# Second model's output weights loaded inside the mixers, output norm by token halves, reordered state space stage, expert gather from a split copy

## Chip, cores and metric

One NeuronCore of one Trainium2 chip runs the whole program. The metric is the device time of one execution in microseconds (us), the median over the runs shown. PE is TensorE, DVE is VectorE, ACT is ScalarE, POOL is GpSimd and SP the engine that issues most DMAs.

## What is computed

A block of a state space and convolution mixer with an expert lookup, and then two layers of a second model, for 256 tokens of 1024 columns. Three places matter here.

```
# first block: state space mixer (16 heads of 64 in 4 groups, state 128, both directions)
dt = softplus(dt_raw + dt_bias);  a = -exp(a_log) * dt
y  = (C B^T * exp(segsum(a))) (x*dt)  +  C state * exp(cumsum a)  +  x * d_skip
o  = group_rmsnorm(y * silu(z)) * ssd_norm

# second model, for l in 0, 1
x = x + concat(ya, yb, yc) @ w_out[l]                    # rwkv, attention, gmlp
h = rms_norm(x, ffn_norm_g[l])
x = x + swiglu(h)            if l == 0
x = x + moe_swiglu(h)        if l == 1                   # 8 experts, 2 per token
# moe: logits = h @ router; top 2; gates = softmax; each expert only over its own tokens
```

## The kernel before

The program is a chain of stages with a barrier of all engines between them (class Stage, L105 to L119): inp, ssd, hy, route, exp, final, then for each of two layers z (norm and input projection), rw (stage_mixers), omix (stage_project_norm, L1354) and dense (l = 0) or moe (l = 1). Within a stage each engine has its own instruction list, written out by hand, and waits on semaphores; the order in those lists sets the order of the work. SP's list is a queue too: a DMA behind a wait is issued after it.

**ssd** (stage_ssd, L659). SP loads two tables for dt and a_log, the triangular masks tri, d_skip and the norm row (L705 to L709). PE turns 10 blocks of the convolved input (L723), while DVE makes softplus and a (L892 to L915); then PE makes the cumulative sums (L733) and the same as rows, once for output partitions 0 and once for 32 (L740). DVE weights x into xw (L930). Then PE: state_of(0), gates_of(0), the row sums of heads 0 and 2, off_of(0), and a loop over 16 heads: sums_of broadcasts the rows of a later head, DVE's head_in makes a difference, ACT its exponential, DVE's head_mask the matrices Mf and Mb (L953, L954), and PE's head_out multiplies them with xw (L784). All heads of a group of 4 collect in one bank py. group_out (L975) adds it to the skip term (L979, which frees py), adds the state's part and multiplies with z; it stands behind the masks of head 4g + 5. At the end the squares, one root, and eight scalings (L1018) go before four blocks of transposes (L814) and copies (L884).

**rw** (stage_mixers, L2109) holds three tiles X, Y and Z3 for the attention. After the last values product (L2319, semaphore m_o_psum) X, Y and Z3 hold nothing that is read again.

**omix** (stage_project_norm). SP loads w_out in two halves of 2 MB, each after the one before has landed (L1375). PE multiplies oT with each half for both token halves: four pieces of 8 products of 512 columns (L1388), an fp32 product being two instructions. DVE adds each to x_tok (L1426). After all four come the squares of both token halves (L1407), the root, the scaling to xn (L1444), 16 transposes (L1397) and 8 scalings to hT (L1454).

**moe** (stage_moe, L2863). Start: SP loads the router, stores x_tok to the output rows, loads three tables and the first two weight blocks (L2951 to L2958). PE's router products (L2981) and DVE's work wait for all four tables. DVE finds the top 2, each token's slot, the list of passes (L3174 to L3197), and then the matrix Pg of ones and zeros that picks the tokens of a pass (L3202). PE gathers them: xn times Pg in fp32 (L2999), over 8 row blocks and 2 token halves. DVE multiplies with the norm gain into hE (L3207), ACT makes its high part hEh (L3079) and DVE the low part hEl (L3212). A pass streams 84 weight blocks through a ring of 21: ACT makes the high part, DVE the low part (fp32r, a 32 bit type for which a product is one instruction), and PE makes six products of 512 columns with each (L3019, L3037). Near its end it gathers the next pass's tokens. Nine passes run.

## Time and profile before

| | us |
|---|---|
| median of 3 runs | 3401.13 |
| lowest, highest | 3394.55, 3401.63 |
| profiled execution, its own time | 3392.16 |
| its span, first to last instruction | 3390.3 |
| ssd stage | 117 |
| omix0, omix1 | 49, 50 |
| moe before its first expert product | 34 |
| moe from there to the end | 1114 |

The page's part 1 has the busy time of each engine, part 4 the chain of work that ended last, followed back from the last instruction. In the timeline the bracket gives the idle time of the engine before an instruction and what released it. PEclk is the granted TensorE clock: 1.0 is 2.4 GHz, 0.5 is 1.2 GHz. The forms print fp32r operands of products as f32; L3019, L3037 and L2008 have fp32r operands, L2999 and all of ssd and omix fp32.

### The profile page before, as it was taken

The numbers are of one execution on the slowest core, as the hardware profiler recorded it, in microseconds if no ns is written. First come the engines' busy times: TensorE is split into PE (matmuls) and PEld (weight loads), VectorE is DVE, ScalarE is ACT, GpSimd is POOL, SyncE is SP. The second block draws the span as 40 slices with busy tenths as digits, with TensorE's granted clock in tenths as the row PEclk, the third lists the DMA queues.
The fourth block names the chain that finished last, engine by engine and source line by source line (L and its number), as shares of the span: only waits on it lengthen the run. The fifth ranks groups of instructions, "written<-read, shape, count | busy, mean of one in ns | idle before, by whom it ended". The sixth has DMA issues, their size and how long they took to land. (4 is left out here: it accounts for less than half of the span.)

```text
span 3390.3 us, 49857 instructions
## 1 busy us (share of the span) xinstructions
PE 3086.4 (91%) x17008; PEld 2570.3 (76%) x17009; DVE 2437.8 (72%) x3650; ACT 1755.2 (52%) x2184; POOL 41.5 (1%) x47
## 2 busy tenths in 40 slices
PE   7998798888899999977879987779999999999997
PEld 3796546888788999965849866648888888888886
DVE  3665663889788666658635467539889999998996
ACT  3343203436533444435224344128888887887886
POOL 0000000000000000000000000000000000000000
PEclk9998698999999999988989988879999999999999
DMA  7560143444577766521045240059999999999994
GB/s 273 203 225 29 40 165 106 133 150 180 218 247 223 220 212 212 187 114 46 1 178 180 104 150 1 31 214 377 376 349 379 372 355 379 362 364 358 386 360 179
DMA packets 225854, 731.95 MB, mean 216 GB/s; under 512 B 23527, under 2 KB 59800, under 8 KB 222872
## 3 DMA queue, kind: packets, MB, share of 16 engines
q1 hardware_dynamic: 221784, 702.32, 56.8%
q0 software_dynamic: 2768, 23.59, 2.4%
q10 hardware_dynamic: 1152, 4.19, 0.3%
q8 instruction: 74, 1.21, 0.1%
q14 instruction: 76, 0.62, 0.1%
HBM read 702.24 MB, written 28.84 MB: 216 GB/s over the span
## 5 line engine op out<-in xcount | busy, mean ns | idle before, releaser
L3216 DVE TENSOR_TENSOR moe_lo<-moe_raw,moe_hi 128x1024 fp32r<-128x1024 f32 x756 | 886.0, 1220 | 55.3 <-ACT moe_hi L3069 36.1
L3069 ACT ACTIVATE moe_hi<-moe_raw 128x1024 fp32r<-128x1024 f32 x756 | 788.1, 1061 | 147.9 <-PE moe_pB L3019 78.0
L3019 PE MATMUL moe_pB<-moe_hi,moe_hEh 128*128 128x512 f32 x1008 | 399.7, 397 | 3.8 <-DVE moe_hEl L3212 3.8
L3019 PE MATMUL moe_pB<-moe_hi,moe_hEl 128*128 128x512 f32 x1008 | 394.1, 391 | 0.0
L3019 PE MATMUL moe_pB<-moe_lo,moe_hEh 128*128 128x512 f32 x1008 | 393.5, 390 | 0.0
L1531 PE MATMUL route_pS<-fh,route_uh 128*128 128x256 f32 x640 | 191.3, 299 | 35.4 <-DVE route_ul L1634 35.1
L3019 PEld LDWEIGHTS moe_pB<-moe_hi,moe_hEh 128*128 128x128 f32 x1008 | 190.0, 188 | 41.6 <-issue 4.0
L3019 PEld LDWEIGHTS moe_pB<-moe_hi,moe_hEl 128*128 128x128 f32 x1008 | 189.7, 188 | 40.7
L3019 PEld LDWEIGHTS moe_pB<-moe_lo,moe_hEh 128*128 128x128 f32 x1008 | 190.1, 189 | 37.9
L1866 PE MATMUL exp_pO<-exp_vh,exp_ah 128*128 128x512 f32 x512 | 201.0, 393 | 4.4 <-DVE exp_al L1925 4.4
L1866 PE MATMUL exp_pO<-exp_vl,exp_ah 128*128 128x512 f32 x512 | 200.6, 392 | 0.0
L1866 PE MATMUL exp_pO<-exp_vh,exp_al 128*128 128x512 f32 x512 | 199.9, 390 | 0.0
L3037 PE MATMUL moe_pB<-moe_hi,moe_ah 128*128 128x512 f32 x504 | 197.0, 391 | 0.0
L3037 PE MATMUL moe_pB<-moe_hi,moe_al 128*128 128x512 f32 x504 | 196.2, 389 | 0.0
L3037 PE MATMUL moe_pB<-moe_lo,moe_ah 128*128 128x512 f32 x504 | 196.1, 389 | 0.0
L1889 ACT ACTIVATE exp_vh<-exp_vs 128x1024 fp32r<-128x1024 f32 x128 | 135.2, 1056 | 116.5 <-PE exp_pO L1866 94.3
L1914 DVE TENSOR_TENSOR exp_vl<-exp_vs,exp_vh 128x1024 fp32r<-128x1024 f32 x128 | 156.3, 1221 | 41.2 <-ACT exp_vh L1889 39.7
L1531 PE MATMUL route_pS<-fl,route_uh 128*128 128x256 f32 x640 | 185.2, 289 | 0.0
L1531 PE MATMUL route_pS<-fh,route_ul 128*128 128x256 f32 x640 | 185.0, 289 | 0.0
L1531 PEld LDWEIGHTS route_pS<-fh,route_uh 128*128 128x128 f32 x640 | 126.8, 198 | 40.2 <-DVE route_ul L1634 29.9
L1854 PE MATMUL exp_pS<-fh,exp_ul 128*128 128x256 f32 x512 | 144.9, 283 | 0.0
L1854 PE MATMUL exp_pS<-fl,exp_uh 128*128 128x256 f32 x512 | 144.9, 283 | 0.0
(742 smaller groups left out, 6738.8 us busy)
## 6 DMA issues: line engine op xcount, KB each, us to landing
moe_raw<-in_moe_w SPq DMA_DIRECT2D x758, 512.0 KB, 6.4
exp_vs<-in_peer_v SPq DMA_DIRECT2D x128, 512.0 KB, 4.6
route_us<-in_peer_u SPq DMA_DIRECT2D x64, 512.0 KB, 3.5
exp_us<-in_peer_u SPq DMA_DIRECT2D x64, 512.0 KB, 5.2
inp_w<-in_w_mod SPq DMA_DIRECT2D x48, 512.0 KB, 6.2
inp_w<-in_w_tiles SPq DMA_DIRECT2D x40, 512.0 KB, 6.0
gates<-route_big POOLq DMA_DIRECT2D x8, 2048.0 KB, 7.5
exp_gs<-gates SPq DMA_DIRECT2D x32, 512.0 KB, 5.8
```

The lines of the kernel that those rows point to most:

```text
L1531: m = pe.matmul(pS[:, n % 2, 0:T], w, x[:, kd], start=kd == 0 and q == 0, stop=kd == KD - 1 and q == 2)
L1854: m = pe.matmul(pS[:, j % 2, 0:T], w, x[:, kd], start=kd == 0 and q == 0, stop=kd == KD - 1 and q == 2)
L1866: m = pe.matmul(pO[:, a, h], w[:, j % RING, ts], x, start=False, stop=False, skip_group_check=True)
L1889: act.activation(vh[:, j % RING], vs[:, j % RING], ACT.Copy).then_inc(vh_ready, 1)
L1914: dve.tensor_tensor(vl[:, j % RING], vs[:, j % RING], vh[:, j % RING], ALU.subtract).then_inc(vl_ready, 1)
L3019: i = pe.matmul(pB[:, kind], l[:, kd], m[:, n % HALVES, ns], start=kd == 0 and x == 0, stop=kd == KD - 1 and x == 2)
L3037: i = pe.matmul(pY[:, h], l[:, u], m[:, n % HALVES, hs], start=g == 0 and u == 0 and x == 0, stop=g == GROUPS - 1 and u == UNITS - 1 and x ...
L3069: act.activation(hi[:, n % HALVES], raw[:, n % RING], ACT.Copy).then_inc(hi_ready, 1)
L3216: dve.tensor_tensor(lo[:, n % HALVES], raw[:, n % RING], hi[:, n % HALVES], ALU.subtract).then_inc(lo_ready, 1)
```

## The change

- ssd: the dt, a_log and d_skip tables are loaded in the inp stage; tri is the stage's first load. gates_of(0) stands among the first transposes, DVE's gates(0) behind a. The row sums go in pairs to partitions 0 and 32. state_of(0) comes after the sums of heads 0 and 2, off_of(0) after head 1. The read of py is a function of its own (inner), ahead of the mask of the next group's first head. The first three groups are normed before the last group's output, and transposed as each is ready.
- mixers and omix: X, Y and Z3 become parts of one allocation that lives until omix ends, and w_out is loaded into it once m_o_psum is reached. The new stage_omix goes by token halves: the four pieces in the order of the token half, each token half squared, normed, turned and scaled by itself, the transposes of the first one between pieces 3 and 4. The scalings of the transposed blocks are shared by DVE and ACT. In layer 1 the norm gain is multiplied into xn as a row, and the transposed blocks are only copied.
- moe: xn, which now has the gain in it, is split once into xh and xl (fp32r), a second matrix Pz is made in fp32r, and the gather is the sum of the products of xh and xl with Pz. hE and its product fall out. The router has a semaphore of its own; the store of x_tok comes after the first two weight blocks; the first Pg and Pz are made before the pass list.

```diff
+                for dst, src in tables["loads"]:
+                    sp.dma_start(dst, src).then_inc(tables["loaded"], 16)
...
-        sp.dma_start(dtb[:], dt_bias.rearrange("a b h -> (a b h)").partition_broadcast(P)).then_inc(dt_loaded, 16)
-        sp.dma_start(alog[:], a_log.rearrange("a b h -> (a b h)").partition_broadcast(P)).then_inc(dt_loaded, 16)
         sp.dma_start(tr[:], tri).then_inc(tri_loaded, 16)
-        sp.dma_start(dskip[:], d_skip.rearrange("a h -> (a h)").partition_broadcast(P)).then_inc(nrm_loaded, 16)
         sp.dma_start(nrm[:], norm.rearrange("a h -> (a h)").partition_broadcast(P)).then_inc(nrm_loaded, 16)
...
+        def gates_of(g):
+            if g:
+                pe.wait_ge(state_ready, g + 1)
+            for s in range(TT):
+                i = pe.matmul(pg[:, s * T:(s + 1) * T], xbcT[:, 8 + g, s * P:(s + 1) * P], xbcT[:, 12 + g, 0:T], start=True, stop=True)
+            i.then_inc(g_psum, 1)
...
+            if n == 1:
+                gates_of(0)
...
-        for base in (0, 32):
-            for d, half, terms in ((0, 0, [(LE, 0)]), (0, 1, [(None, 0), (LE, 1)]), (1, 1, [(GE, 1)]), (1, 0, [(GE, 0), (None, 1)])):
-                at = d * T + half * P
-                for nt, (which, src) in enumerate(terms):
+        for d, half, terms in ((0, 0, [(LE, 0)]), (0, 1, [(None, 0), (LE, 1)]), (1, 1, [(GE, 1)]), (1, 0, [(GE, 0), (None, 1)])):
+            at = d * T + half * P
+            for nt, (which, src) in enumerate(terms):
+                for base in (0, 32):
                     i = pe.matmul(prow[base:base + HEADS, at:at + P], a[:, src, d * HEADS:(d + 1) * HEADS],
                                   k.ones[:] if which is None else tr[:, which], start=nt == 0, stop=nt == len(terms) - 1)
...
         def state_of(g):
             pe.wait_ge(xw_ready, 1 + g // 2)
+            pe.wait_ge(g_ready, max(g, 1))
             if g == 0:
                 pe.wait_ge(x_read, 10)
-            else:
-                pe.wait_ge(g_ready, g)
+            if g == 1:
+                pe.wait_ge(state_ready, 1)
             for s in range(TT):
                 i = pe.matmul(pg[:], btok[:, s, g, :], xw[:, TT + s, g].rearrange("p d n -> p (d n)"), start=s == 0, stop=s == TT - 1)
             i.then_inc(state_psum, 1)
-        def gates_of(g):
...
-        state_of(0)
-        gates_of(0)
         pe.wait_ge(row_ready, 1)
         pe.wait_ge(ea_ready, 1)
         pe.wait_ge(na_cum, 1)
         sums_of(0)
         sums_of(2)
-        off_of(0)
+        state_of(0)
...
-            if h % HPG == 1 and g:
+            if h % HPG == 1:
                 off_of(g)
...
-            pe.wait_ge(o_ready, n // 2 + 1)
+            pe.wait_ge(o_ready, n + 1)
...
-        keep_state(0)
...
+            if h == 0:
+                keep_state(0)
...
+        act.wait_ge(mean_ready, 1)
+        act.activation(rt[:, 0:LAST], ms[:, 0:LAST], ACT.Sqrt).then_inc(root_ready, 1)
         squares(GROUPS - 1)
-        act.wait_ge(mean_ready, 1)
-        act.activation(rt[:], ms[:], ACT.Sqrt).then_inc(root_ready, 1)
+        act.wait_ge(mean_ready, 2)
+        act.activation(rt[:, LAST:], ms[:, LAST:], ACT.Sqrt).then_inc(root_ready, 1)
...
+        gates(0)
...
+        def inner(g):
+            dve.wait_ge(y_psum, (g + 1) * HPG)
+            dve.tensor_tensor(y[:, :, g * H4:(g + 1) * H4], py[:].rearrange("p (l n) -> p l n", l=TT), xd[:], ALU.add).then_inc(py_read, 1)
...
-        dve.wait_ge(nrm_loaded, 32)
-        skipped(0)
-        gates(0)
+        dve.wait_ge(nrm_loaded, 16)
         head_in(0)
...
             if hh == 0 and g:
                 gates(g)
+                inner(g - 1)
             head_mask(h)
+            if h == 0:
+                skipped(0)
...
+        def normal(first, last, cols):
+            dve.wait_ge(squared, last * TT)
+            dve.tensor_scalar(ms[:, cols], ss[:, cols], 1.0 / H4, EPS, ALU.mult, ALU.add).then_inc(mean_ready, 1)
+            dve.wait_ge(root_ready, 1 if first == 0 else 2)
+            c.link(dve.reciprocal(rs[:, cols], rt[:, cols]))
+            for g in range(first, last):
+                gs = slice(g * H4, (g + 1) * H4)
+                for l in range(TT):
+                    i = dve.scalar_tensor_tensor(out=y[:, l, gs], in0=y[:, l, gs], scalar=rs[:, g * TT + l:g * TT + l + 1],
+                                                 in1=nrm[:, gs], op0=ALU.mult, op1=ALU.mult)
+                i.then_inc(o_ready, 1)
+
+        normal(0, GROUPS - 1, slice(0, LAST))
+        inner(GROUPS - 1)
         group_out(GROUPS - 1)
...
+        normal(GROUPS - 1, GROUPS, slice(LAST, TT * GROUPS))
...
+        sp.wait_ge(q["m_o_psum"], 1)
+        for h in range(2):
+            sp.dma_start(w_out[:, h], w_tiles[h]).then_inc(w_loaded, 16)
...
+PIECES = [(a, h) for a in range(TT) for h in range(2)]
...
+        pe.wait_ge(w_loaded, 32)
+        for a, h in PIECES:
+            for kd in range(KD):
+                i = pe.matmul(pm[a][h][:], oT[:, kd, a * P:(a + 1) * P], w[:, h, kd], start=kd == 0, stop=kd == KD - 1)
+            i.then_inc(mix_psum, 1)
+            if (a, h) == (1, 0):
+                turned(0)
+        turned(1)
...
+    @block.vector
+    def _(dve):
+        c = Chain(dve, ch)
+
+        def added(n):
+            a, h = PIECES[n]
+            hs = slice(h * BANK, (h + 1) * BANK)
+            dve.wait_ge(mix_psum, n + 1)
+            dve.tensor_tensor(x_tok[:, a, hs], pm[a][h][:], x_tok[:, a, hs], ALU.add).then_inc(x_ready, 1)
+
+        def normed(a):
+            dve.wait_ge(squared, 2 * a + 2)
+            c.link(dve.tensor_tensor(xms[:, a:a + 1], xss[:, a, 0:1], xss[:, a, 1:2], ALU.add))
+            dve.tensor_scalar(xms[:, a:a + 1], xms[:, a:a + 1], 1.0 / D, EPS, ALU.mult, ALU.add).then_inc(mean_ready, 1)
+            dve.wait_ge(root_ready, a + 1)
+            c.link(dve.reciprocal(xrs[:, a:a + 1], xrt[:, a:a + 1]))
+            dve.wait_ge(x_ready, 2 * a + 2)
+            if row is None:
+                dve.tensor_scalar(xn[:, a], x_tok[:, a], xrs[:, a:a + 1], None, ALU.mult).then_inc(xn_ready, 1)
+            else:
+                dve.wait_ge(row_loaded, 16)
+                dve.scalar_tensor_tensor(out=xn[:, a], in0=x_tok[:, a], scalar=xrs[:, a:a + 1], in1=rowt[:],
+                                         op0=ALU.mult, op1=ALU.mult).then_inc(xn_ready, 1)
+
+        def scaled(a):
+            dve.wait_ge(t_psum, 2 * a + 1)
+            if row is not None:
+                i = dve.tensor_copy(hT[:, 0:4, a * P:(a + 1) * P], pt[0][:].rearrange("p (j t) -> p j t", t=P))
+            else:
+                for kd in range(4):
+                    i = dve.tensor_scalar(hT[:, kd, a * P:(a + 1) * P], pt[0][:, kd * P:(kd + 1) * P], scales[:, kd:kd + 1], None, ALU.mult)
+            i.then_inc(t_read_dve, 1)
+
+        added(0)
+        added(1)
+        normed(0)
+        added(2)
+        scaled(0)
+        added(3)
+        normed(1)
+        scaled(1)
...
-        sp.dma_start(rw[:], router).then_inc(loaded, 16)
-        sp.dma_start(rows[0:T].rearrange("(a p) d -> p a d", p=P), x_tok[:]).then_inc(x_kept, 16)
+        sp.dma_start(rw[:], router).then_inc(rw_loaded, 16)
...
+        sp.dma_start(rows[0:T].rearrange("(a p) d -> p a d", p=P), x_tok[:]).then_inc(x_kept, 16)
...
-        pe.wait_ge(loaded, 64)
+        pe.wait_ge(rw_loaded, 16)
...
+        pe.wait_ge(loaded, 48)
...
-                for a in range(TT):
-                    i = pe.matmul(pX[:, half, n * P:(n + 1) * P], xn[:, a, kd * P:(kd + 1) * P], Pg[:, a], start=a == 0, stop=a == TT - 1)
+                for x, src in enumerate((xh, xl)):
+                    for a in range(TT):
+                        i = pe.matmul(pX[:, half, n * P:(n + 1) * P], src[:, a, kd * P:(kd + 1) * P], Pz[:, a],
+                                      start=x == 0 and a == 0, stop=x == 1 and a == TT - 1)
...
+        pe.wait_ge(xl_ready, 1)
...
+        act.activation(xh[:], xn[:], ACT.Copy).then_inc(xh_ready, 1)
...
-            act.wait_ge(hE_ready, p + 1)
-            act.activation(hEh[:], hE[:], ACT.Copy).then_inc(hEh_ready, 1)
+            act.wait_ge(gather_psum, 2 * p + 2)
+            act.activation(hEh[:].rearrange("p k t -> p (k t)"), pX[:].rearrange("p b n -> p (b n)"), ACT.Copy).then_inc(hEh_ready, 1)
...
-        dve.wait_ge(loaded, 64)
+        dve.wait_ge(xh_ready, 1)
+        dve.tensor_tensor(xl[:], xn[:], xh[:], ALU.subtract).then_inc(xl_ready, 1)
+        dve.wait_ge(loaded, 48)
...
+        def gather_matrix(p):
+            for a in range(TT):
+                dve.tensor_scalar(Pg[:, a], io[:], slot[:, a, bass.ds(p, 1)], None, ALU.is_equal)
+                i = dve.tensor_scalar(Pz[:, a], io[:], slot[:, a, bass.ds(p, 1)], None, ALU.is_equal)
+            i.then_inc(pg_ready, 1)
...
+        gather_matrix(0)
...
-            dve.tensor_tensor(hE[:].rearrange("p (b k) t -> p b k t", b=2), pX[:].rearrange("p b (k t) -> p b k t", k=4),
-                              scales.rearrange("p (b k) -> p b k", b=2).unsqueeze(3).to_broadcast([P, 2, 4, P]), ALU.mult).then_inc(hE_ready, 1)
...
-            dve.tensor_tensor(hEl[:], hE[:], hEh[:], ALU.subtract).then_inc(h_ready, 1)
+            dve.tensor_tensor(hEl[:].rearrange("p k t -> p (k t)"), pX[:].rearrange("p b n -> p (b n)"),
+                              hEh[:].rearrange("p k t -> p (k t)"), ALU.subtract).then_inc(h_ready, 1)
...
-        gather_matrix(0)
...
+    shared = keep(heads, f"heads{l}", [P, 3 * 2 * BHEADS * T], "right")
+    w_out = shared[:, 0:2 * KD * BANK].rearrange("p (h k n) -> p h k n", h=2, k=KD)
+    w_loaded = nc.alloc_semaphore(f"w_out_loaded{l}")
```

## Rows read from the trace of the kernel before

**Rows 1.** Page, part 4: chain that ended last, shares of the span by engine
```profile
PE 33%; DMA 0%; DVE 0%; ACT 0%; issue 0%; SPq 0%; ACTq 0%; POOL 0%; POOLq 0%; DVEq 0%
```

**Rows 2.** Windows by stage: us, PE, PEld, DVE, ACT, POOL busy, PEclk, DMA share, GB/s
```profile
295.70:412.70 117.00, 89.77 (x380) 60.65 (x380) 76.66 (x162) 40.42 (x90) 0.00 (x0) 0.68 0.02 8
...
2191.10:2241.30 50.20, 33.46 (x80) 15.73 (x80) 7.91 (x16) 2.50 (x5) 0.00 (x0) 0.83 0.23 84
2241.30:2275.20 33.90, 18.28 (x78) 15.86 (x78) 13.91 (x68) 5.99 (x7) 1.51 (x3) 0.57 0.97 371
...
2397.00:2518.70 121.70, 121.70 (x570) 101.40 (x569) 110.50 (x106) 98.88 (x103) 2.16 (x2) 1.00 0.97 367
```

**Rows 3.** Timeline of omix0: start us, us, engine line op out<-in xcount [idle before <-releaser]
```profile
1699.24 8.24 SPq L1375 DMA_DIRECT2D omix_w<-in_w_out  x2
...
1707.19 29.27 PE L1388 MATMUL omix_pm<-omix_w,oT 128*128 128x512 f32 x64 [11.22 <-DMA omix_w<-in_w_out]
...
1744.93 1.73 DVE L1454 TENSOR_SCALAR hTf<-omix_pt,cols 128x256 f32<-128x256 f32 x4 [0.36 <-PE omix_pt L1397]
```

**Rows 4.** Timeline of omix1, its two weight loads (the second waits for the first)
```profile
2191.97 9.34 SPq L1375 DMA_DIRECT2D omix_w<-in_w_out  x2
```

**Rows 5.** Timeline of the mixers of layer 0, PE, last values products
```profile
1642.42 0.61 PE L2319 MATMUL rw_p<-rw_mla_v,rw_mla_y 128*128 128x64 f32 x4
```

**Rows 6.** Timeline of the state space stage, DVE, to head 0's second matrix
```profile
299.80 0.48 DVE L892 TENSOR_TENSOR ssd_u<-ssd_p,ssd_dtb 128x32 f32<-128x32 f32 x4 [12.44 <-DMA ssd_alog<-in_ssd_a_log]
...
301.35 0.36 DVE L900 COPY ssd_mf<-ssd_tri 128x128 f32<-128x128 f32 x2 [0.61 <-DMA ssd_tri<-in_tri]
...
327.65 0.68 DVE L954 TENSOR_TENSOR ssd_Mb<-ssd_ex,ssd_gb 128x512 f32<-128x512 f32 x1
```

**Rows 7.** Timeline of the state space stage, PE, sums and row sums
```profile
309.35 0.60 PE L733 MATMUL ssd_p<-ssd_a,ssd_tri 128*128 128x16 f32 x4
...
310.77 0.56 PE L740 MATMUL ssd_p<-ssd_tri,ssd_a 128*16 128x128 f32 x2
...
314.40 0.38 PE L740 MATMUL ssd_p<-ones,ssd_a 128*16 128x128 f32 x2
```

**Rows 8.** Timeline of the state space stage, PE, first head of groups 1 and 2
```profile
346.00 0.66 PE L784 MATMUL ssd_py<-ssd_xw,ssd_Mf 128*128 128x64 f32 x2 [5.04 <-DVE fT L979]
...
367.28 0.66 PE L784 MATMUL ssd_py<-ssd_xw,ssd_Mf 128*128 128x64 f32 x2 [2.90 <-DVE fT L979]
```

**Rows 9.** Timeline of the state space stage, its end
```profile
399.34 0.69 DVE L979 TENSOR_TENSOR fT<-ssd_py,ssd_xd 128x512 f32<-128x512 f32 x1 [4.04 <-PE ssd_py L784]
...
406.15 3.25 DVE L1018 SCALAR_TENSOR_TENSOR fT<-fT,ssd_rs,ssd_nrm 128x256 f32<-128x256 f32 x8
...
411.75 0.60 ACT L884 ACTIVATE oT<-ssd_p 128x512 f32<-128x512 f32 x1 [0.26 <-PE ssd_p L814]
```

**Rows 10.** Timeline of the expert stage up to its first product
```profile
2248.64 7.00 PE L2981 MATMUL moe_pX<-moe_rw,hTf 128*128 128x8 f32 x32 [3.87 <-DMA moe_tr<-in_tri]
...
2264.77 0.48 DVE L3202 TENSOR_SCALAR moe_Pg<-moe_io,moe_slot 128x128 f32<-128x128 f32 x2
...
2265.31 6.11 PE L2999 MATMUL moe_pX<-moe_Pg,xnf 128*128 128x128 f32 x32 [5.28 <-DVE moe_Pg L3202]
...
2271.45 1.23 DVE L3207 TENSOR_TENSOR moe_hE<-moe_pX,cols 128x1024 f32<-128x1024 f32 x1 [3.53 <-PE moe_pX L2999]
...
2275.26 0.79 PE L3019 MATMUL moe_pB<-moe_hi,moe_hEh 128*128 128x512 f32 x1 [3.85 <-DVE moe_hEl L3212]
```

**Rows 11.** Timeline of PE, first half of one gather
```profile
2389.94 1.95 PE L2999 MATMUL moe_pX<-moe_Pg,xnf 128*128 128x128 f32 x16
```

**Rows 12.** Chain in order of time: start us, us, products of one group
```profile
2300.64 5.44 PE moe_pB L3037 x24
```

**Rows 13.** Line L2999, weight loads: count, duration ns min/median/max
```profile
L2999 PEld LDWEIGHTS moe_pX<-moe_Pg,xnf x320: 187/192/333, 2265.3 to 3367.4; 128*128 128x128 f32 x160
```

**Rows 14.** Line L3019, weight loads of fp32r operands
```profile
L3019 PEld LDWEIGHTS moe_pB<-moe_hi,moe_hEh x1008: 187/188/331, 2275.3 to 3357.2; 128*128 128x128 f32 x168
```

More of the change, by code:

```diff
@@ L656, with stage_ssd @@
 LOG1P_TERMS = 9
-def stage_ssd(nc, k, dt_bias, a_log, d_skip, norm, tri, xbcT, z_tok, dtT, xtok, ytok, oT):
+def stage_ssd(nc, k, tables, norm, tri, xbcT, z_tok, dtT, xtok, ytok, oT):
     LE, GE, LT, GT = range(4)
@@ L2874, in stage_moe @@
+def stage_moe(nc, k, router, iota, tri, w, hT, xn, x_tok, rows, out):
     KINDS, UNITS = 3, 4
@@ L3610, in second_layer @@
         else:
-            stage_moe(nc, k, a["router"], a["iota"], a["tri"], a["moe_w"], hT, xn, k.col(f"ffn{l}"), x_tok, a["moe_rows"], out)
+            carried.close()
+            stage_moe(nc, k, a["router"], a["iota"], a["tri"], a["moe_w"], hT, xn, x_tok, a["moe_rows"], out)
 def kernel(**inputs):
```

144 lines of the change are left out of this document (92 added, 52 removed).

## Prediction

> **What bounds it now.** I read the chain that ended last first: TensorE (PE) alone holds it [rows 1], and all of that third of the span lies in the expert stage. Then the windows by stage. In one expert pass PE is busy 121.70 of 121.70 us, DVE 110.50, ACT 98.88, DMA 0.97 of the time [rows 2]: PE bounds the nine passes, with DVE and DMA close. The stages that the change touches besides are not bound by one engine: state space takes 117.0 us with PE busy 89.8 at a mean clock of 0.68 and DVE 76.7, the expert start 33.9 us with PE 18.3 [rows 2]. There the timelines say what each wait ends on. The profiled execution took 3392.2 us (span 3390.3); the median of the runs is 3401.1, nine above it. The sum is made against 3392.2 and carried over to the median.
>
> **omix0 and omix1.** SP issues the output weights at 1699.24, PE starts at 1707.19 [rows 3]; with the weights in SBUF PE starts where SP now issues: -8.0. In omix1 the first load is issued at 2191.97 and the second, which waits for the first to land as PE does, 9.0 later (9.34 less its own 0.33) [rows 4]: -9.0. The new loads wait for the last values product, done by 1643.03 [rows 5]; omix0 starts at about 1698.3, so 4 MB have 55 us where the old stage needed about 8 us for each half. SP has nothing queued behind that wait. PE started at the lower clock before and does so after: 0, or up to 2 us either way per stage. The tail: the products end at 1707.19 + 29.27 = 1736.46, the last hT piece at 1746.66 [rows 3], 10.2 us of adds, squares, root, scaling and transposes over both token halves. Afterwards only the second half is left behind the last product: 5.4 us by halving each long operation (add, square, scale) and keeping the short ones. PE does the first half's eight transposes ahead of the last 6.9 us of products, 8 x 0.11 = 0.9. So -3.9 each (-2 to -5). In omix1 the gain row makes the scaling a two-input operation (+0.5) and merges four scalings into one copy (-0.4). Both stages: -8.0 - 9.0 - 2 x 3.9 = **-24.8**, between -20 and -29.
>
> **State space.** Its first DVE operation waits until 299.80 for the a_log table; the masks then wait until 301.35 for tri [rows 6]. The three tables come with the front stage, where SP only gives 3 more small issues in a queue that mostly waits for ring space. Tri becomes the first load and the chain to the decay moves up 1.4 (0.5, if tri needs as long as now, to 2.8). The row sums, 24 instructions from 310.77 to 314.78 [rows 7], go in neighbouring pairs to output partitions 0 and 32, which may overlap: -2 (0 to -2). The sums of heads 0 and 2 no longer stand behind the state product, its copy and the gates, which are computed earlier; DVE's own weighting ends 1.4 earlier, and head 0's matrices, ready at 328.33 [rows 6], come some 10 us earlier. PE does not keep that: state 0, two heads, state 1 and the state's contribution of group 0 now stand between, mostly at the low clock. Adding them (2.9, 2 x 2.6, sums 1.9, 3.4, 3.4, then 1.35 + 0.9 + 1.1 + 1.35 at the high one) from 315.4 on gives head 3 out at 337, the drained bank and head 4's matrices (0.7 + 1.3) at 339, against 346.00 [rows 8]: -7. In the later groups PE waited 2.90 until the bank was drained, behind two mask pairs [rows 8]; draining comes first now, but then waits for the heads of the group before and delays the mask by 0.7: -0.8 for each of two groups. The end: 13.0 us from the last product's drain at 399.34 to 412.35 [rows 9]. Six of the eight scalings (3.25 x 6/8 = 2.4) and the table load move into the 4.04 us that DVE idled; they overrun it by 0.6. Left: 8.9, so -4.1. Sum 7.0 + 1.6 + 4.1 = **-12.7**, between -5 (PE stays at the low clock through group 0) and -19.
>
> **Expert start.** The router products waited 3.87 us, for tri, queued behind 1 MB of x_tok [rows 10]; they need only the router now, and x_tok goes behind the first two weight blocks. I take -2.8, as their low parts on DVE come next. ACT's split copy and DVE's subtraction over 2048 columns (2 x 1.2 us) run while DVE waited for the same tables. PE waited 5.28 us for the gather matrix [rows 10]; the pass list (4 us of small operations) moves behind it, while four comparisons instead of two (0.48 for two [rows 10]) stay: -3.7. The gather, 6.11 us because its end ran at the high clock, runs fully at the low one: +0.9. The 1.23 us product with the scales falls out [rows 10]: -1.2. Sum **-6.8**, between -3 and -11. The weight ring starts the passes with some 15 blocks instead of 20 in it, still enough, as SP's waits in the passes are for ring space, not the reverse. POOL's wait for x_tok ends long before its first scatter.
>
> **The gather in the passes** is the disputed price. Before: 16 fp32 products are 32 instructions, two halves of 16 in 1.95 us [rows 11]. Sixteen of 128 columns in 1.95 and four of 16 columns in 0.60 [rows 7] give the same spacing: 1.35/12 = 0.112 us, whatever the columns. So the weight load sets it. After: 32 fp32r instructions. Their load lasts 188 ns as that of the fp32 ones, 192 [rows 13, 14], and 24 fp32r products of 512 columns take 5.44 us, 227 each [rows 12], 13 more than 512/2.4 = 213. The trace has no fp32r product under 256 columns, so I bound it: below by 128/2.4 + 13 = 66 ns, above by four trips of the columns, 213 + 13 = 227. I take 112 to 120, by the equal loads: 0 to +0.26 per pass, **+1** in nine passes. DVE loses 1.23 and gains two comparisons (0.5) per pass, under PE. The Trainium skill, "TensorE: Matmul & The Clock Gate", section "Back-to-back issue gap", has a stream of load and product at 128 columns settle at about 81 ns; by it the gather would fall by 32 x 31 ns, 1 us a pass. The rows of this trace stand at 112 for fp32.
>
> **Sum.** -24.8 - 12.7 - 6.8 + 1 = -43, so 3349 for the profiled kind of execution and **3358 us** for the median.
>
> **Rivals.**
> (a) *Light loads*: fp32r weights load faster than rows 14 suggest, 66 ns per instruction: 9 x 32 x 0.046 = -13, and -3 in the first gather, 3342. The Trainium skill, "TensorE: Matmul & The Clock Gate", section "Weight-path perf modes", has the fast weight load on for 128 weights that are not FP32; fp32r may be such a type. Against: the equal load durations.
> (b) *Narrow fp32r runs at a quarter rate*: 227 ns. 9 x 32 x 0.115 = +33 and up to +4 in the first gather, so -6 in all: 3395, no change. For it: nothing narrower than 256 was ever split here. Against: no row.
> (c) *The clock*: the gather now streams half the columns per instruction (one trip of 128, not two), and PE in the state space stage fell to the low clock with thin products, to a mean of 0.68 [rows 2]. If it falls in each gather, 1.5 to 3 us a pass: +13 to +27, about 3378. Against: the gather is 4 us between products of 512 columns.
> (d) *The other side, slower*: narrow fp32r at a quarter rate with its weight load not hidden, 227 + 107 = 334 ns. 9 x 32 x 0.222 = +64, +6 at the start: 3401 - 44 + 70 = 3427. It decides from 0.112 + 44/320 = about 250 ns per gather instruction on. For it: PE is bound, so every ns shows. Against: all fp32r loads in the trace hide.
> (e) *The change does less than it says*: PE at the low clock in omix and group 0, tri late: all terms at their small ends, -28 + 3, 3376.
>
> **Chances.** Forecast 0.55, (a) 0.12, (b) 0.11, (c) 0.08, (d) 0.04, (e) 0.10. A measurement here can tell about 0.2% (7 us) from no change. Of (b), 0.02 falls faster, 0.08 within and 0.01 slower. Faster 0.55 + 0.12 + 0.08 + 0.10 + 0.02 = 0.87, same 0.08, slower 0.04 + 0.01 = 0.05. The range runs from 3336 (the forecast with its large ends, (a) in it) to 3382 ((e), and most of (c)); (b) and (d) are left out, 0.15.
>
> **What would show it.** omix0 and omix1: first product under 1 us behind the barrier, no wait for weights, 5 to 6 us from last product to end; stages of about 37 us. State space near 104 us, head 4 some 7 us earlier, scalings between head 15's matrices and the last drain. Expert start 27 us. A pass of 121.7 to 122.0 with 32 gather instructions: 112 to 120 ns apart says the load sets it, 66 to 81 says (a), 227 or a doubled count says (b), 334 (d), a clock of 0.5 in the passes (c). The forecast falls if the pass changes by over 1 us, or if omix still shows a wait for DMA.

## The result and the profile after

The changed kernel took 3351.16 us (median of 4 runs, 3345.71 to 3357.79), the kernel before on the same chip 3398.49: a ratio of 0.9862, with a 95% interval of 0.984 to 0.9884, 47 us. The profiled execution took 3357.79 us (span 3356.1), the slowest of the four. Against the 3392.16 of before it gained 34.4 us only, so a part of the gain lies in what differs from one execution to the next. A later series gave 3350.60 against 3396.11, 45.5 us.

The chain that ended last is still PE's [rows 1], with the same 33% of the span.

The windows of the same stages, columns as in [rows 2] (state space, omix1, expert start, one pass):

```profile
296.00:402.70 106.70, 89.15 (x380) 61.25 (x380) 76.98 (x164) 40.03 (x91) 0.00 (x0) 0.69 0.02 8
2174.60:2212.30 37.70, 32.11 (x80) 15.06 (x80) 7.57 (x14) 4.49 (x12) 0.00 (x0) 0.91 0.04 14
2212.30:2241.30 29.00, 16.63 (x79) 14.29 (x79) 15.23 (x70) 7.99 (x8) 1.51 (x3) 0.56 0.92 348
2362.00:2483.64 121.64, 121.64 (x570) 101.38 (x569) 109.68 (x107) 99.17 (x103) 1.84 (x2) 1.00 0.97 366
```

By the barriers between the stages (the windows are rounded), state space takes 106.70 us instead of 116.92, omix0 37.36 instead of 48.66, omix1 37.70 instead of 50.24, the expert start 28.95 instead of 33.97, a pass 121.64 instead of 121.706. Together -39.7, of -34.4 in all: some 5 us came back elsewhere (dense +2.4 and route +1.3, which the change does not touch, norm and mixers of layer 1 +1.8). The stages vary by that much from one execution to the next: in the two executions of before, dense took 199.8 and 202.0 us. So 34.4 us is not the gain, and the medians are what counts.

**omix**, its timeline, with the load of w_out as SP issues it in the mixers of layer 0 (answers to [rows 3]):

```profile
1633.74 0.80 SPq L2263 DMA_DIRECT2D heads<-in_w_out  x2
```

```profile
1689.97 22.92 PE L2915 MATMUL omix_pm<-heads,oT 128*128 128x512 f32 x48 [3.33 <-PEq L119]
...
1713.60 7.03 PE L2915 MATMUL omix_pm<-heads,oT 128*128 128x512 f32 x16
...
1720.67 0.69 DVE L2953 TENSOR_TENSOR x_tok<-omix_pm,x_tok 128x512 f32<-128x512 f32 x1 [6.02 <-PE omix_pm L2915]
...
1724.90 1.14 ACT L2928 ACTIVATE hTf<-omix_pt,cols 128x128 f32<-128x128 f32 x4 [2.17 <-PE omix_pt L2909]
```

PE starts 1.0 us behind the barrier at 1688.99, with no wait for a transfer. Its last product ends at 1720.63, the last hT piece at 1726.04: 5.4 us, as the prediction had it, instead of 10.2. omix1 has 6.2, as its last eight transposes ran at the low clock (1.91 us for them, 1.09 in omix0):

```profile
2209.48 1.91 PE L2909 MATMUL omix_pt<-ident,xnf 128*128 128x128 f32 x8 [3.67 <-DVE xnf L2966]
...
2211.43 0.60 ACT L2930 ACTIVATE hTf<-omix_pt 128x512 f32<-128x512 f32 x1 [3.52 <-PE omix_pt L2909]
```

In the one execution where they ran at the high clock there (below, output weights in omix again), the tail of omix1 is 5.4 us too.

**State space**, PE and DVE, to the first head of group 1 (answers to [rows 7, 8]) and at the end (to [rows 9]):

```profile
311.65 0.62 PE L749 MATMUL ssd_p<-ssd_tri,ssd_a 128*16 128x128 f32 x4
...
313.76 0.64 PE L749 MATMUL ssd_p<-ones,ssd_a 128*16 128x128 f32 x4
...
340.65 0.69 PE L789 MATMUL ssd_py<-ssd_xw,ssd_Mf 128*128 128x64 f32 x2 [2.08 <-DVE ssd_Mb L972]
```

```profile
391.38 2.46 DVE L1030 SCALAR_TENSOR_TENSOR fT<-fT,ssd_rs,ssd_nrm 128x256 f32<-128x256 f32 x6
...
393.76 0.68 DVE L983 TENSOR_TENSOR fT<-ssd_py,ssd_xd 128x512 f32<-128x512 f32 x1
...
401.82 0.60 ACT L890 ACTIVATE oT<-ssd_p 128x512 f32<-128x512 f32 x1 [0.26 <-PE ssd_p L817]
```

The row sums take 2.75 us for 24 instructions (311.65 to 314.40), the first head of group 1 starts 44.6 us behind the barrier instead of 50.3, and the waits of 5.04 and 2.90 are now 2.08, for the masks and not for the bank. (In the nine other executions of this code that head starts 38.4 to 41.7 us behind the barrier.) The last drain starts at 393.76, the stage's work ends at 402.42: 8.7 us.

**Expert start** (answers to [rows 10]):

```profile
2216.46 3.75 PE L3108 MATMUL moe_pX<-moe_rw,hTf 128*128 128x8 f32 x32
...
2222.11 1.06 ACT L3205 ACTIVATE moe_hi<-moe_raw 128x1024 fp32r<-128x1024 f32 x1 [7.07 <-DMA moe_raw<-in_moe_w]
2223.20 2.59 DVE L3289 TENSOR_TENSOR moe_lo<-moe_raw,moe_hi 128x1024 fp32r<-128x1024 f32 x2 [5.34 <-ACT moe_hi L3205]
...
2225.71 0.17 DVE L3291 COPY moe_lg<-moe_pX 128x16 f32<-128x16 f32 x1
...
2231.60 0.66 PE L3128 MATMUL moe_pX<-moe_Pz,moe_xh 128*128 128x128 f32 x2 [1.55 <-DVE moe_Pz L3310]
...
2239.83 1.23 DVE L3346 TENSOR_TENSOR moe_hEl<-moe_pX,moe_hEh 128x1024 fp32r<-128x1024 f32 x1 [1.48 <-ACT moe_hEh L3211]
...
2241.29 0.79 PE L3149 MATMUL moe_pB<-moe_hi,moe_hEh 128*128 128x512 f32 x1 [2.63 <-DVE moe_hEl L3346]
```

The router's products no longer wait. But they end at 2220.21, and DVE reads them at 2225.71: its queue has the first two low parts ahead, and those wait for the first weight block. They stood there before the change too, as two rows of that trace show:

```profile
2252.82 2.50 DVE L3155 TENSOR_TENSOR moe_lo<-moe_raw,moe_hi 128x1024 fp32r<-128x1024 f32 x2 [3.62 <-ACT moe_hi L3073]
...
2255.67 0.17 DVE L3157 COPY moe_lg<-moe_pX 128x16 f32<-128x16 f32 x1 [0.35 <-PE moe_pX L2981]
```

There the low parts ended at 2255.32, and DVE waited only 0.35 us more for the router's products.

**The gather** in a pass and its weight loads (answers to [rows 11, 13]):

```profile
2356.36 0.33 PE L3128 MATMUL moe_pX<-moe_Pz,moe_xh 128*128 128x128 f32 x2
...
2358.10 0.62 PE L3156 MATMUL moe_pT<-ident,moe_prod 128*128 128x128 f32 x4
```

```profile
L3128 PEld LDWEIGHTS moe_pX<-moe_Pz,moe_xh x160: 187/192/333, 2231.6 to 3333.0; 128*128 128x128 f32 x160
```

Sixteen fp32r products in 2358.10 - 2356.36 = 1.74 us, 109 ns each on average and mostly 112 from one to the next, the spacing of the fp32 ones. The clock is at 1.0 throughout. From the first gather product of a pass to the expert product behind the last one are 3.93 us, before the change (2389.94 to 2393.87) and after (2356.36 to 2360.29).

### The profile page after: what moved, and what is told of

It reads as the page before. It is cut to its first block and busy times, and to the rows that moved or that the text cites. A ratio compares the mean times of both kernels' runs of the same rounds, so it can differ in the third digit from the quotient of the medians.

```text
span 3356.1 us, 49912 instructions
## 1 busy us (share of the span) xinstructions
PE 3086.5 (92%) x17008; PEld 2574.3 (77%) x17009; DVE 2430.1 (72%) x3665; ACT 1762.9 (53%) x2206; POOL 39.8 (1%) x47
## 5 line engine op out<-in xcount | busy, mean ns | idle before, releaser
L1882 PE MATMUL exp_pO<-exp_vh,exp_al 128*128 128x512 f32 x512 | 199.8, 390 | 0.0
```

Of the source, the lines that this page charges most:

```text
L1882: m = pe.matmul(pO[:, a, h], w[:, j % RING, ts], x, start=False, stop=False, skip_group_check=True)
```

## The experiments

All are edits of the changed kernel. Nine with a question of their own come first, then two executions for comparison and a version put together.

**Row sums apart.**

```diff
-for d, half, terms in (...):
+for base, d, half, terms in [(base, *t) for base in (0, 32) for t in (...)]:
     at = d * T + half * P
     for nt, (which, src) in enumerate(terms):
-        for base in (0, 32):
...
```

> The changed kernel with the row sums of the state space stage in their old order (all for output partitions 0, then all for 32). In the changed kernel the 24 of them took 2.75 us at the low clock, 115 ns apart, where single fp32 instructions at that clock stand 213 apart. Theory: neighbours that write to partitions 0 and 32 overlap, so undone they take about 24 x 0.213 = 5.1 us at the low clock (or some 4.0 if the clock rises in between), and head 0 of group 1 and the stage come 1.3 to 2.4 us later. Rival: a short instruction costs half as much in any order there; then the stage stays within 0.3 us of 106.7.

PE's timeline, first and last row sums:

```profile
310.82 0.61 PE L749 MATMUL ssd_p<-ssd_tri,ssd_a 128*16 128x128 f32 x2
...
314.61 0.64 PE L749 MATMUL ssd_p<-ones,ssd_a 128*16 128x128 f32 x2
```

4.43 us (310.82 to 315.25) instead of 2.75, both at the low clock, so neighbours for partitions 0 and 32 do overlap: in the changed order the two of a pair start 7 ns apart and the next pair 213 ns after the first. The Trainium skill, "TensorEngine Tiling (Array Packing)", section "Key Properties", says that different tiles can execute in parallel; these rows agree. The stage, though, took 102.90 us, and three executions of the unedited stage with the same mean clock of 0.71 took 102.59, 102.60 and 103.26. The 1.7 us were gone by the first head of group 1 (41.35 us behind the barrier, 41.2 to 41.7 in those three), so what the pairs gained for the stage is too small to be measured. The rival's 0.3 us around 106.7 was set on one execution; against the right neighbours the stage did not change. The clock mattered more than the order: in the second execution of the kernel before, the old order ran at the high clock and took 2.37 us.

**Bank read late again.**

```diff
 if hh == 0 and g:
     gates(g)
-    inner(g - 1)
...
 if hh == 1 and g:
+    inner(g - 1)
     group_out(g - 1)
```

> The changed kernel with the read of py behind the mask of head 4g + 5 again. Theory: that read is what PE waits for at each of the three group changes, and it now comes two pairs of mask and difference later: PE's wait of 2.08 us in front of heads 4, 8 and 12 grows to 2.9 or more, the stage by 0.8 to 1.7 us at each change, 3 to 5 in all, to about 111. Rival: PE's clock and the exponentials set the pace of the groups, and the read is hidden: the stage within 1 us of 106.7.

```profile
337.96 0.41 PE L789 MATMUL ssd_py<-ssd_xw,ssd_Mf 128*128 128x64 f32 x2 [3.26 <-DVE fT L983]
...
358.06 0.41 PE L789 MATMUL ssd_py<-ssd_xw,ssd_Mf 128*128 128x64 f32 x2 [2.90 <-DVE fT L983]
...
378.18 0.66 PE L789 MATMUL ssd_py<-ssd_xw,ssd_Mf 128*128 128x64 f32 x2 [2.90 <-DVE fT L983]
```

The waits grew from 2.08 to 3.26, 2.90 and 2.90, 2.8 us in sum, as the theory had it. The stage took 102.56 us at a mean clock of 0.72. The executions of the unedited stage at 0.73 took 99.8 to 100.5, those at 0.71 took 102.6 to 103.3, so between them about 101.3 would be due: 1 to 1.5 us is left of the 3 to 5 expected. From the first product of head 4 to the last product of the stage this execution took 51.36 us, and two of the unedited stage with the same clock there (0.70) took 49.80 and 49.85: the two later waits cost what they grew by, 1.64. So the theory had the waits right and the price of each (0.8 to 1.7 us) too high; and the rival, that the read is hidden, is wrong by this comparison.

**Output weights in omix again.**

```diff
-sp.wait_ge(q["m_o_psum"], 1)
-for h in range(2):
-    sp.dma_start(w_out[:, h], w_tiles[h]).then_inc(w_loaded, 16)
...
+for h in range(2):
+    sp.dma_start(w[:, h], w_tiles[h]).then_inc(w_loaded[h], 16)
...
-pe.wait_ge(w_loaded, 32)
+if a == 0:
+    pe.wait_ge(w_loaded[h], 16)
```

> The changed kernel with both halves of w_out issued at the start of omix0 and omix1 instead of in the mixers, one semaphore for each half, the work by token halves kept. Theory: PE starts 8 us later and the second half, issued at once behind the first, lands within PE's 7 us of the first piece: omix0 and omix1 each 8 to 9 us longer, 45.5 to 46.5 us. Rival: the transfer in the mixers slows something there or in the stage before; then the mixers of this run are shorter than 165.4 and 181.3 us, by up to several us, and what was gained in omix is partly only moved.

omix0 took 45.28 us (+7.9) and omix1 46.90 (+9.2). SP and PE in omix0:

```profile
1684.90 0.81 SPq L2895 DMA_DIRECT2D heads<-in_w_out  x2
...
1693.00 22.40 PE L2915 MATMUL omix_pm<-heads,oT 128*128 128x512 f32 x48 [11.38 <-DMA heads<-in_w_out]
```

The first half needs 8.1 us, and the second is there in time. The mixers took 166.99 and 176.69 us, values that executions with the load in the mixers also had (167.01 and 176.75): moving the 4 MB there cost nothing that can be seen. (Those executions vary, from 165.4 to 169.4 and from 176.7 to 181.3 us, so a cost of a us or two would be seen only in such close pairs.)

**Norm of both halves behind the last product.**

```diff
-        if (a, h) == (1, 0):
-            turned(0)
+    turned(0)
     turned(1)
...
-    act.wait_ge(x_ready, n + 1)
+    act.wait_ge(x_ready, 4)
...
-added(0); added(1); normed(0); added(2); scaled(0); added(3); normed(1); scaled(1)
+added(0); added(1); added(2); added(3); normed(0); normed(1); scaled(0); scaled(1)
```

> The changed kernel with nothing of the norm started before the fourth piece (weights still loaded in the mixers). Theory: what stands behind the last product is again all of squares, root, scalings, 16 transposes and their copies: 10 us instead of 5.4 (omix0) and 6.2 (omix1), less the 0.9 of transposes that PE no longer does ahead: both stages 3 to 4.5 us longer, 40.5 to 42. Rival: with ACT and DVE sharing the copies the tail is short in any order, and the stages grow by less than 2.

omix0 41.21 us (+3.9), omix1 40.48 (+2.8). The end of omix0:

```profile
1718.21 0.69 DVE L2951 TENSOR_TENSOR x_tok<-omix_pm,x_tok 128x512 f32<-128x512 f32 x1 [6.17 <-PE omix_pm L2915]
...
1727.28 1.14 ACT L2927 ACTIVATE hTf<-omix_pt,cols 128x128 f32<-128x128 f32 x4 [2.87 <-PE omix_pt L2909]
```

From the last product (its add starts at 1718.21) to 1728.42 are 10.2 us, just the tail of before. So the gain in the tail is that of the work by token halves. In omix1 it is less, as there the tail of the changed kernel is 6.2.

**Gather with 64 columns.**

```diff
-for x, src in enumerate((xh, xl)):
...
+pieces = [(0, P)] if n % 2 == 0 else [(0, P // 2), (P // 2, P)]
+for lo_, hi_ in pieces:
+    for x, src in enumerate((xh, xl)):
...
```

> The changed kernel with every second block of the gather done in two halves of 64 columns: 16 instructions of 128 columns and 32 of 64 in a gather, the result the same. Theory: the weight load sets the spacing, whatever the columns (110 to 112 ns): the gather takes 48 x 0.111 = 5.3 us instead of 4.1, and as PE bounds the passes each is 1.8 us longer, 123.4, the kernel 16 us. Rival: the columns set it: 64 columns 55 to 66 ns apart, the gather 3.6 to 4.1 us as before, the pass 121.6.

One pass, and eight instructions of 64 columns (x2 four times) in a gather:

```profile
2360.00:2483.46 123.46, 123.46 (x585) 103.16 (x585) 109.70 (x106) 99.18 (x103) 1.77 (x2) 1.00 0.96 361
```

```profile
2351.22 0.36 PE L3130 MATMUL moe_pX<-moe_Pz,moe_xh 128*128 128x64 f32 x2
...
2352.09 0.42 PE L3130 MATMUL moe_pX<-moe_Pz,moe_xh 128*128 128x128 f32 x2
```

2352.09 - 2351.22 = 0.87 us for eight, 109 ns on average at 64 columns as at 128. The pass took 123.46 us (+1.82), the execution 3368.59. So the columns do not set the spacing. That the weight load does fits, as each instruction has one of its own, but it was not varied here. The row sums of the state space stage have loads of 16 columns instead of 128; in the second execution of the kernel before they ran at the high clock:

```profile
L740 PEld LDWEIGHTS ssd_p<-ssd_tri,ssd_a x16: 92/97/97, 310.3 to 312.1; 128*16 128x16 f32 x16
```

Their loads take 97 ns instead of 192, and their fp32 products of 128 columns still start 109 ns apart. So for fp32 at 128 columns a shorter load does not shorten the spacing; for fp32r, what sets it stays open. The Trainium skill, "TensorE: Matmul & The Clock Gate", section "Back-to-back issue gap", has about 81 ns at 128 columns; the trace differs, and it decides.

**Gather in fp32.**

```diff
-for x, src in enumerate((xh, xl)):
-    for a in range(TT):
-        i = pe.matmul(pX[...], src[:, a, ...], Pz[:, a], ...)
+for a in range(TT):
+    i = pe.matmul(pX[...], xn[:, a, ...], Pg[:, a], ...)
...
-act.activation(xh[:], xn[:], ACT.Copy).then_inc(xh_ready, 1)
```

> The changed kernel with the gather in fp32 from xn and Pg again (the gain still multiplied into xn before; no xh, xl, Pz). Theory: an fp32 product is two instructions of the same spacing as one fp32r instruction, so the pass is the same within 0.1 us (121.64), and the expert start the same or up to 1 us shorter, since four comparisons become two (0.4) and DVE's xl (2.3 us) was hidden. Rival: the split gather saves PE time: then a pass with the fp32 gather is longer by 0.5 us or more.

The pass is 121.71 us again (+0.07), the start 26.89, 1.4 to 2.2 less than with the split gather (28.29 to 29.12 in the others), more than the theory's 0 to 1. Two comparisons fewer are 0.5 of it. The rest is the clock, which rose inside this gather, as in both executions of before; it took 5.67 us instead of 7.06:

```profile
2223.50 5.67 PE L3126 MATMUL moe_pX<-moe_Pg,xnf 128*128 128x128 f32 x32 [1.07 <-DVE moe_Pg L3301]
```

**Low parts later.**

```diff
-for n in range(PRE):
-    dve.wait_ge(hi_ready, n + 1)
-    dve.tensor_tensor(lo[:, n], raw[:, n], hi[:, n], ALU.subtract).then_inc(lo_ready, 1)
 dve.wait_ge(l_psum, 1)
...
 gather_matrix(0)
+for n in range(PRE):
+    dve.wait_ge(hi_ready, n + 1)
+    dve.tensor_tensor(lo[:, n], raw[:, n], hi[:, n], ALU.subtract).then_inc(lo_ready, 1)
```

> The changed kernel with DVE's low parts of the first two weight blocks behind the gather matrix instead of ahead of the read of the router's products. In the changed kernel the router's products end at 2220.2, DVE reads them at 2225.7, because it waits for the first block (landed 2222.1) and makes two low parts. Theory: the read comes at once, everything up to the first expert product moves 5.4 us forward: the start takes 23.5 us instead of 28.95. Rival: the first weight blocks are late anyway, or their low parts stand in front of the last step: less than 3 us gained, and the first expert product waits for a low part.

```profile
2216.38 0.17 DVE L3288 COPY moe_lg<-moe_pX 128x16 f32<-128x16 f32 x1 [1.96 <-PE moe_pX L3108]
...
2229.38 1.02 ACT L3211 ACTIVATE moe_hEh<-moe_pX 128x1024 fp32r<-128x1024 f32 x1 [8.24 <-PE moe_pX L3128]
...
2231.57 1.23 DVE L3346 TENSOR_TENSOR moe_hEl<-moe_pX,moe_hEh 128x1024 fp32r<-128x1024 f32 x1 [0.25 <-DVE moe_meta L3330]
...
2233.03 0.79 PE L3149 MATMUL moe_pB<-moe_hi,moe_hEh 128*128 128x512 f32 x1 [3.68 <-DVE moe_hEl L3346]
```

The router's products are read 7.9 us behind the barrier (2208.47) instead of 13.4, and the first expert product starts at 24.56 us, 4.4 earlier (5.4 expected; the rival had less than 3). The missing 1.1 us is a new wait: the low part of the gathered tokens (2231.57) now starts behind the gates' arithmetic on DVE, 1.17 us after ACT's high part ended at 2230.40.

**Store of x_tok first.**

```diff
 sp.dma_start(rw[:], router).then_inc(rw_loaded, 16)
+sp.dma_start(rows[0:T]..., x_tok[:]).then_inc(x_kept, 16)
...
-sp.dma_start(rows[0:T]..., x_tok[:]).then_inc(x_kept, 16)
```

> The changed kernel with the store of x_tok (1 MB) ahead of the three tables and the first weight blocks, as before the change; the router's own semaphore is kept. Theory: the store takes DMA time ahead of the first block, which lands 2 to 4 us later, and DVE's read of the router's products behind it: the start 2 to 4 us longer than 28.95. Rival: the router's semaphore alone gave the gain; the start within 0.5 us of 28.95.

```profile
2213.45 1.17 SPq L3085 DMA_DIRECT2D moe_raw<-in_moe_w  x2
...
2218.27 1.06 ACT L3205 ACTIVATE moe_hi<-moe_raw 128x1024 fp32r<-128x1024 f32 x1 [6.88 <-DMA moe_raw<-in_moe_w]
```

The start is 28.74 us, unchanged. The weight blocks are issued 4.8 us behind the barrier (2208.69) instead of 2.2 to 2.6, and ACT has the first at 9.6 us. In the other eleven executions it had it at 8.9 to 10.4 us, in the two of before at 9.6 and 10.4. The rival was right. Why an earlier issue brings no earlier landing stays open.

**PE kept at work.**

```diff
 i.then_inc(l_psum, 1)
+for n in range(8):
+    pe.matmul(pY[:, n % 2], k.zero[:], hT[:, 0:2, :], start=True, stop=True)
...
 i.then_inc(rank_psum, 1)
+for n in range(1):
+    pe.matmul(pY[:, n % 2], k.zero[:], hT[:, 0:2, :], start=True, stop=True)
```

> The changed kernel with PE kept at work in the expert start: eight more zero products of 512 columns between the router's products and the ranks (where PE waited 7.5 us), and one between the ranks and the gather (where it waited 1.55 us). They write zeros where zeros already stand. Theory: PE was at the low clock through the ranks (2.3 us) and the gather (7.06 us) because it had only waited or streamed 8 columns at a time before; with the 512-column products the clock is at 1.0 there, the ranks take 1.2 us and the gather 3.6 to 4.1: the start 3.5 to 4.5 us shorter than the 28.3 to 28.95 us of the runs so far. Rival: the clock falls again in the ranks and in the wait behind them; the gather still takes over 6 us and the start is the same within 0.5 us, or up to 0.5 longer.

```profile
2219.33 0.28 PE L3115 MATMUL moe_pX<-moe_chosen,moe_tr 128*128 128x8 f32 x2
...
2226.71 1.02 ACT L3215 ACTIVATE moe_hEh<-moe_pX 128x1024 fp32r<-128x1024 f32 x1 [10.26 <-PE moe_pX L3132]
...
2229.07 1.23 DVE L3350 TENSOR_TENSOR moe_hEl<-moe_pX,moe_hEh 128x1024 fp32r<-128x1024 f32 x1 [0.25 <-DVE moe_meta L3334]
```

The clock did most of what the theory said: the ranks took 1.2 us instead of 2.3, and the gather 4.6 instead of 7.06 at a mean clock of 0.79, not the 3.6 to 4.1 of a clock of 1.0. The start, 27.96 us, hardly moved, as the rival had it, for another reason. The eight products overran, so that the ranks began 2.0 us late, and the low part of the tokens waited 1.3 us for the gates' arithmetic on DVE. These two took back 3.3 of the 3.6 us gained on PE.

**The kernel before, once more.**

> The kernel before the change, unchanged, to see what its state space stage does in another execution. In seven executions of one and the same code of the changed stage it took 96.96 to 106.70 us, and the longer the clock was low in it (46.8 to 67.1 us) the longer it took, about 0.48 us for each us. Theory: the stage of before has the same swing (116.92 us with 74.4 us low was near its long end), so another execution may well give a shorter one, on a line of the same slope: 110 to 117 us. Rival: the old order holds the clock down always: within 1 us of 116.9. The passes, omix and the expert start stay within 0.3 us of 121.71, 48.7, 50.2 and 34.0 in either case.

```profile
295.98:410.57 114.59, 85.65 (x380) 57.92 (x380) 76.50 (x162) 40.18 (x90) 0.00 (x0) 0.72 0.02 8
```

114.59 us instead of 116.92, mean clock 0.72 instead of 0.68. That lies in the expected 110 to 117, but not on the expected line: 10.2 us less at the low clock (64.3 instead of 74.5) were worth 2.3 us, 0.23 for each. The passes (121.71) and the expert start (34.17) repeated within 0.2 us, omix0 (49.2) and omix1 (49.7) to about half a us, where 0.3 was expected.

**The changed kernel, once more**, five rounds.

> The changed kernel, unchanged, as the measure for the next run and to see which of its profile's stages repeat. Theory: omix0 37.4, omix1 37.7, the pass 121.64 and the gather of the start 7.06 repeat within 0.2 us (omix0 within 0.6), the expert start within 0.7; the state space stage does not, and lands between 97 and 107 us on a line with the time at the low clock. Median 3346 to 3357 us. Rival: the 106.7 us of its first profile is the rule, and the shorter ones of the experiments came from their edits.

Median 3350.60 us (3348.72 to 3351.57) against 3396.11, ratio 0.9864 (0.9849 to 0.9879). omix0 37.87, omix1 37.70, expert start 29.12, pass 121.64, all as expected. The rival, that 106.7 us is the rule for the state space stage, is refuted. That stage here, and the same code at its fastest, in the kernel with the weights loaded in omix:

```profile
295.90:396.50 100.60, 81.64 (x380) 55.78 (x380) 77.02 (x164) 39.95 (x91) 0.00 (x0) 0.73 0.03 9
```

```profile
297.71:394.68 96.97, 80.69 (x380) 55.00 (x380) 77.06 (x164) 40.07 (x91) 0.00 (x0) 0.76 0.03 9
```

In all twelve executions of the changed kernel and its edits, time and mean clock of this stage go together:

| mean clock | stage, us | stage code |
|---|---|---|
| 0.76 | 96.97 | changed |
| 0.73 | 99.76, 99.83, 99.88, 99.94, 100.54 | changed |
| 0.71 | 102.59, 102.60, 103.26 | changed |
| 0.69 | 106.70 | changed |
| 0.72 / 0.71 | 102.56 / 102.90 | bank read late / row sums apart |
| 0.72 / 0.68 | 114.59 / 116.92 | before |

So order and clock can be told apart in part. Before, with 64.3 us at the low clock, the stage took 114.59; between its executions with 60.4 us (103.26) and 67.1 (106.70) the changed stage would take about 105.3 (an estimate from these rows). Some 9 us are the new order at an equal clock. The other 5 of the mean difference go with less time at the low clock, 56 us on average instead of 69; two executions of before are too few to say that this belongs to the change.

**A start put together**: the low parts later and the gather in fp32, as in the two edits above, two zero products ahead of the ranks and one behind them, and the gates' arithmetic (choices) last.

```diff
-choices()
 gathered(0)
+choices()
```

> The changed kernel with the expert start put together from what the runs showed: low parts of the first two blocks behind the gather matrix, the gates' arithmetic behind the low part of the gathered tokens, the gather in fp32 as before the change, two zero products in PE's wait before the ranks and one behind them. Theory: router read at 7.9 us, gather from about 13.7 for 4 to 5.7 us, its two parts 2.4 us more: the first expert product 21 to 22.5 us behind the barrier instead of 28.3, the pass 121.71 (+0.6 in nine), the kernel 5 to 7 us below the changed one. Rival: the gates' arithmetic now delays the third block's low part and the token numbers, PE waits in the first pass instead, and less than 3 us is left.

```profile
2214.25 0.17 DVE L3284 COPY moe_lg<-moe_pX 128x16 f32<-128x16 f32 x1 [2.32 <-PE moe_pX L3107]
...
2219.80 3.84 PE L3130 MATMUL moe_pX<-moe_Pg,xnf 128*128 128x128 f32 x32
...
2226.23 1.22 DVE L3341 TENSOR_TENSOR moe_hEl<-moe_pX,moe_hEh 128x1024 fp32r<-128x1024 f32 x1 [0.22 <-DVE moe_passi L3333]
...
2227.69 0.49 PE L3150 MATMUL moe_pB<-moe_hi,moe_hEh 128*128 128x512 f32 x1 [4.05 <-DVE moe_hEl L3341]
...
2232.88 0.19 PEld L3150 LDWEIGHTS moe_pB<-moe_hi,moe_hEh 128*128 128x128 f32 x1 [1.03 <-DVE moe_lo L3346]
```

The start is 21.72 us, 7.4 less than in the run beside it, the gather 3.84 at the high clock. The median is 3342.01 us (3339.49 to 3344.57) against 3350.60 (3348.72 to 3351.57) for the changed kernel in the same series; the runs do not overlap, and the difference is 8.6 us where 5 to 7 were expected. Against before the ratio is 0.9838 (0.9824 to 0.9851). The rival showed in small: PE waits 0.59 us in the first pass for a low part, and the low part of the tokens still stands 1.5 us behind the pass list.

## Why the prediction was right, point by point

The forecast was -43 us; the two series have -47.3 and -45.5, inside the range. The total came out nearer than its terms. As measured over the executions they are about -23.8, -14.5, -5.4 and -0.6, together -44; the state space stage and the gather gave 1.8 and 1.6 us more than forecast, omix and the expert start 1.0 and 1.4 less, and that these cancel is luck. The forecast for the profiled kind of execution, 3349, missed by 9 us (3357.79), as that one had the slowest state space stage of ten and the 5 us in other stages. What the profiles give for each term:

| term | predicted | profile after | what the runs add |
|---|---|---|---|
| omix weights | -17.0 | | 7.9 + 9.2 = 17.1 when undone |
| omix tail | -7.8 | | 3.9 + 2.8 = 6.7 when undone |
| omix both | -24.8 | -23.8 | |
| state space | -12.7 | -10.2 | mean -14.5 over executions |
| expert start | -6.8 | -5.0 | -4.9 to -5.7 |
| gather, nine passes | +1 | -0.6 | pass 121.71 in fp32, 121.64 split |

- **omix.** Both mechanisms stood, each within 1.2 us, and the two add up: 23.8. The small miss is in omix1's tail, where I took the short operations at the high clock.
- **State space.** The sum was near, and its parts were not. Two parts were undone by themselves, the row sums and the early bank read; the early tables, the order of group 0 and the norm by groups were not, so for them the cause is argued from the timelines. The -12.7 was worked on one execution of before, taken as if its stretches of low clock belonged to the order of the work. The same code took 96.97 to 106.70 us. The ten executions of the changed stage have a mean of 101.2 us, the two of before 115.8: -14.5. The first profile of after happened to be the slowest. The first of the cumulative sums starts 9.8 to 10.0 us behind the barrier in ten executions and 11.0 and 11.3 in two, against 12.25 and 11.55 before (forecast 1.4 earlier, between 0.5 and 2.8). Head 4 came 5.7 us earlier in the first profile and 8.6 to 11.9 in the nine other executions (forecast 7.0). The -2 for the row sums came true on PE (-1.7) and was worth nothing at the stage's end; the early bank read is worth 1 to 2 us in all. The end took 8.7 us behind the last drain's start, where 8.9 behind the last product were forecast (9.5 measured; the six scalings overran it by 0.9 and not 0.6, the other 0.3 is in what follows). The working of that part had a gap: of the 4.1 us that it takes off, the scalings (2.4) and the table load (1.28 in the trace), less the overrun of 0.6, make 3.1, and no row stands for the rest.
- **Expert start.** The step that failed is "I take -2.8" for the router's wait. The read came only 1.0 us earlier (13.4 instead of 14.4 behind the barrier). I had named the low parts that come next, and did not follow them to the first weight block, on which both orders wait alike. The trace of before had it: DVE waited 0.35 us for the router's products there, so removing PE's 3.87 us of waiting could give no more than 0.35 (1.14 in the second execution), unless the block came earlier. It came 0.7 us earlier in this execution (ACT has it 9.8 us behind the barrier, 10.4 before), which makes the 1.0. The other steps measured as forecast: gather matrix earlier -3.75 (-3.7), gather at the low clock +0.95 (+0.9), the product with the scales -1.2 (-1.2). Moving x_tok's store was worth nothing.
- **Gather.** "I take 112 to 120, by the equal loads" is what decided, and it was right within 1 to 3 ns: 109 to 112. The reason given, that the load sets the spacing whatever the columns, is borne out for the columns and not shown for the load. Rivals (a) (66 ns), (b) (227) and (d) (334) are excluded by the trace and by the run with 64 columns; (c) by the granted clock, 1.0 through the passes but for the first 5.9 us of the first one (5.1 before). The -0.6 us stays open: the fp32 run gives it back, but the gather itself takes 3.93 us in both forms.
- **Rival (e)**, the small ends of all terms, held for the row sums alone.

## What to carry to other kernels

Where a wait is removed from one engine, follow the queue of the next reader to its own transfer before a gain is counted: here 2.8 us became 1.0, and one reordering on DVE was worth 4.4 more. A transfer that bounds a stage's start and needs only space can be issued in the stage before, if a buffer is dead there; here that gave 17 us and cost nothing that could be seen. A stage that runs partly at the low clock has no single time: look at several executions before a difference of a few us is put down to an edit.

## What the runs showed of the hardware that was not expected

- The same code at the same place took 96.97 to 106.70 us, with a mean granted clock of 0.76 to 0.69. The time moved by about 0.48 us for each us more at the low clock (46.8 to 67.1 us of it): 9.73 / 20.3. In the two executions of before it was 0.23. What sets where the low stretches fall was not tried.
- PE's clock did not follow whether PE had an instruction: in the expert start it rose at the end of the zero products of 512 columns (four instructions, from 0.6 to 4.3 us behind the barrier), and fell again within the 32 router products of 8 columns, which follow without a gap, at 7.5 us; it stayed low through the ranks and the gather. In one execution, with the weights loaded in omix, it did not rise there at all. More zero products of 512 columns ahead of the gather brought it back: 7.06 us became 4.6, and 3.84 together with the fp32 form.
- The two forms of the first gather differ in the clock. The fp32 gather of 32 instructions, all after the same ranks at the low clock, took 6.11, 6.30 and 5.67 us, as the clock rose inside it each time; the fp32r one of 32 instructions took 7.06 in all eight executions, at 0.5 to its end. Why was not tried.
- At the high clock the instructions of products start 109 to 112 ns apart at 64 and at 128 columns, in fp32 (two for each product) and in fp32r (one), and fp32 ones of 128 columns do so also with weights of 16 columns, whose load takes 97 ns instead of 192.
- Row sums for output partitions 0 and 32, in turn, overlap: at the low clock the two of a pair start 7 ns apart, and 24 take 2.75 us; for one of the two alone they stand 213 ns apart.
